# Twenty cache copies move from behind the output projection's weights into the compression stage

## The reference, cut to what matters

```python
kv_all = jnp.concatenate([bufs[g], qkv[:, :, g, 1:3]], axis=1)
new_bufs.append(kv_all[:, kv_all.shape[1] - keep:])
```

## Time and profile before

| what | value |
|---|---|
| three runs | 1793.05, 1796.68, 1798.58 us (median 1796.68) |
| the profiled execution | 1787.76 us, its span 1786.1 us |
| TensorE busy | 1573.9 us (88%), mean granted clock 0.942 |
| VectorE, ScalarE, GpSimd busy | 661.4, 389.7, 203.4 us |
| HBM read, written | 413.88 MB, 192.48 MB |
| share of SP's copy line (L499) in the chain that ended last | 10% |

### The profile page before, as it was taken

One profiled execution on the slowest core, in us unless ns is written; L12 is line 12 of the kernel. 1 busy time (PEld: TensorE's weight loads), 2 busy tenths in 40 slices (PEclk: granted clock), 3 DMA queues, 4 the chain that ended last, 5 costly groups with the idle time before them and its releaser, 6 DMA issues.

```text
span 1786.1 us, 23452 instructions
## 1 busy us (share of the span) xinstructions
PE 1573.9 (88%) x8593; PEld 1276.7 (71%) x8593; DVE 661.4 (37%) x1526; ACT 389.7 (22%) x1179; POOL 203.4 (11%) x301
## 2 busy tenths in 40 slices
PE   6999998999899999999999999999776800889996
PEld 5877787668788888878888878676544600778885
DVE  2256412158823210036767631554655200112001
ACT  1111111133320000026666511453322100000001
POOL 1100000112401000001111100453242000000000
PEclk8899999999999999989999999998899855999998
DMA  5599999999779976687999423201588999999740
GB/s 172 207 354 381 408 383 342 376 366 333 250 142 257 315 253 235 208 137 116 145 139 145 127 76 108 95 1 48 199 300 281 350 329 328 369 373 375 292 141 24
DMA packets 170946, 423.33 MB, mean 237 GB/s; under 512 B 10376, under 2 KB 131536, under 8 KB 168032
## 3 DMA queue, kind: packets, MB, share of 16 engines
q1 hardware_dynamic: 147840, 344.27, 59.2%
q0 software_dynamic: 19312, 67.47, 14.2%
q10 hardware_dynamic: 3696, 10.32, 1.6%
HBM read 413.88 MB, written 192.48 MB: 339 GB/s over the span
## 4 chain that ended last, share of the span: by engine, by line
PE 70%; SPq 12%; DMA 7%; DVE 6%; issue 2%; ACT 1%; POOL 0%; ACTq 0%; DVEq 0%; POOLq 0%
PE bank L621 18%; PE bank L787 13%; SPq L499 10%; PE bank L774 9%; PE bank L703 4%; PE bank L806 2%; PE bank L857 2%; PE bank L854 2%; PE bank L859 2%; DMA a_win_sample<-oT 2%; PE bank L714 2%; PE bank L658 2%; DMA cring<-cache_b_kv 1%; PE bank L751 1%; DMA a_win_sample<-area 1%
## 5 line engine op out<-in xcount | busy, mean ns | idle before, releaser
L621 PE MATMUL bank<-hT,wring 128*128 128x264 f32 (+1 forms) x1488 | 353.7, 393 | 0.5 <-DVE area L1333 0.5
L774 PE MATMUL bank<-hT,wring 128*128 128x264 f32 x1024 | 232.8, 390 | 108.1 <-DMA wring<-mlp_w_up 108.1
L621 PEld LDWEIGHTS bank<-hT,wring 128*128 128x128 f32 (+1 forms) x1488 | 279.1, 192 | 66.8 <-issue 8.2
L774 PEld LDWEIGHTS bank<-hT,wring 128*128 128x128 f32 x1024 | 195.3, 192 | 145.5 <-issue 104.4
L787 PE MATMUL bank<-area,wring 128*128 128x264 f32 x1024 | 228.4, 386 | 2.8 <-DVE area L1285 2.8
L787 PEld LDWEIGHTS bank<-area,wring 128*128 128x128 f32 x1024 | 194.6, 190 | 36.6 <-DVE area L1283 3.6
L1649 ACT ACTIVATE turned<-xT 128x264 f32<-128x264 f32 x40 | 16.9, 423 | 649.9 <-DVE xT L1289 565.1
L1283 DVE SCALAR_TENSOR_TENSOR area<-bank,rv 128x264 f32 x64 | 27.7, 432 | 274.7 <-PE bank L774 274.4
L1289 DVE TENSOR_TENSOR xT<-bank,xT 128x264 f32<-128x264 f32 x16 | 6.9, 432 | 220.3 <-PE bank L787 220.3
L562 POOL TENSOR_SCALAR area<-ident,small 128x128 f32<-128x128 f32 x96 | 56.3, 603 | 179.9 <-DVE small L1366 179.9
L621 PE MATMUL bank<-oT,wring 128*128 128x264 f32 x256 | 61.9, 400 | 0.9 <-DVE oT L1630 0.5
(11 more groups left out here) (311 smaller groups left out, 2319.6 us busy)
## 6 DMA issues: line engine op xcount, KB each, us to landing
a_win_sample<-cache_a_win SPq DMA_DIRECT2D x64, 2047.0 KB, 21.3
wring<-a_w_in SPq DMA_DIRECT2D x36, 1024.0 KB, 13.4
wring<-mlp_w_up SPq DMA_DIRECT2D x32, 1024.0 KB, 13.4
wring<-mlp_w_down SPq DMA_DIRECT2D x32, 1024.0 KB, 5.1
a_win_sample<-cache_a_win SPq DMA_DIRECT2D x16, 2044.0 KB, 20.2
cring<-cache_a_win POOLq DMA_DIRECT2D x24, 1024.0 KB, 11.3
cring<-cache_b_kv POOLq DMA_DIRECT2D x62, 256.0 KB, 6.5
cring<-cache_b_kv SPq DMA_DIRECT2D x50, 256.0 KB, 7.6
```

The source lines that it names most:

```text
L621: mm = pe.matmul(bk[half if bank is None else bank][0:width, 0:R], wring[:, blk % NW, c, half * P:half * P + width], rhs[:, c, :], start=( ...
L774: mm = pe.matmul(bk[half][:, 0:R], wring[:, blk % NW, c, half * P:(half + 1) * P], hT[:, c, :], start=(c == 0), stop=(c == DC - 1))
```

## The change

The copies are issued by a small function, `copies(n)`. After each of SP's eight page groups it takes 3 copies (groups 0 to 3) or 2 (groups 4 to 7) from the list: 12 + 8 = 20. The 20 behind block 86 are gone. The list and its order are the same; so are the last 26 copies, one behind each block from 87 to 112. No wait on a semaphore is added or removed, and no copy is added or left out.

```diff
+            def copies(n):
+
+                for d, s in shifts[:n]:
+                    sp.dma_start(d, s).then_inc(S["copies_done"], 16)
+                del shifts[:n]
+
             def w_block(i):
...
                     cmp_loads(sp, i, range(SP_PAGES), ks_landed)
+                    copies(3 if i < 4 else 2)
                     continue
...
                 elif B_UP0 <= i < B_BIN:
                     n_copies = 1 if i % 3 == 0 else 0
                 else:
-                    n_copies = {B_UP0 - 1: 16, B_UP1 - 1: 20}.get(i, 1 if i >= B_UP1 else 0)
-                for d, s in shifts[:n_copies]:
-                    sp.dma_start(d, s).then_inc(S["copies_done"], 16)
-                del shifts[:n_copies]
-            while shifts:
-                d, s = shifts.pop(0)
-                sp.dma_start(d, s).then_inc(S["copies_done"], 16)
+                    n_copies = {B_UP0 - 1: 16}.get(i, 1 if i >= B_UP1 else 0)
+                copies(n_copies)
+            copies(len(shifts))
```

## The result

The changed kernel takes 1721.2 us (median of four executions, 1712.99 to 1767.02) against 1797.4 us before; the ratio is 0.9565, with a 95% interval from 0.9513 to 0.9617. It is 76 us faster. Some executions of both kernels and of most variants run at a lower granted clock and take longer, so the ratios and the lists of times in the experiments leave them out, and single traces are compared by stages in front of the attention of layer B, where that clock showed (this stretch took 395 to 433 us in four of the traces, 355 to 372 us in the others).

What follows compares the result with a forecast made beforehand. Bound: 20 copies queued on SP ahead of block 87, for which PE idles 99.0 us; DMA engines full in the compression. -112.9 + 79 + 12 = -22 us against the median 1796.7 gives 1775 us, range 1722 to 1803.

Steps and rivals of the forecast that it cites:

- part 1: MLP 1: with the 20 copies gone from behind block 86, its work takes MLP 0's time, -112.9 us.
- the lead of 25 us: MLP 1: block 87 issued 25.2 us before needed; ten large copies shrink this to about 12 us, so nothing waits.
- Part 3: MLP 0: three copies behind page group 0 delay weights up to block 46, 18 - 6 = +12 us of PE wait.
- Part 2: Compression: 15 copies behind page groups 1 to 6 cost 90 us of engine time, partly given back; sum +79 us.
- so I let times add: Compression: DMA engines taken as full (share 1.05, queues 49% each), so copies' 6.0 us each add to the pages' time.
- the hidden rival: Compression: if bytes are the limit, all copies fit beside the pages; 5 to 25 us come back, 1690 to 1709; chance 0.12.
- PE's lower clock after waits: Compression: idle gaps of 11 to 17 us lower PE's clock; hidden in groups 1 to 6, about 4 us in group 7.
- The 8 us given back for POOL's turns: Compression: POOL's page packets in q0 still get turns while copies run in q1, 30 of an engine's 280, about 8 us.
- The 8 us for POOL's window loads: Compression, group 7: POOL's 4 MB window loads take turns with SP's last pages, adding about 8 us.
- The rival in which copies cost over 7.5 us each: Page groups: copies ahead spread the engines; above 7.5 us each the kernel is over 5 us slower; chance 0.14.

## Why the prediction was wrong

**What bounded the kernel, and part 1, were right.** Block 87 stood behind twenty copies, and MLP 1 now runs at the pace of MLP 0: 113.93 us for the up product in one piece, 113.2 us won against 112.9 predicted. A copy behind each block does no harm, as the lead of 25 us said.

**Part 3 was right in size, and only half in its reason.** The three copies behind group 0 cost 12.0 us in this trace, as summed, and PE's largest wait for weights there is 7.2 us, for block 46 as named. That the figure agrees to the digit is luck, given 4 us of scatter in this stretch. And with spread pages the same three copies cost nothing, so the room was taken by the slow pages as much as by the copies.

**Part 2 failed, in one step: "so I let times add", with the pages' time left as it was.** It took the DMA share of 1.05 at 164 GB/s, and the two queues at 49% each, for engines without room, and put the copies' time on top of the pages' 29.3 us. What the runs showed in its place: a page packet's time there is no fixed price. Its packets are held up at their destination of 16 partitions; written to 128 partitions, the same packets need 42% of the engines' time instead of 98%. And with copies among them pages move faster than pages alone, even while no copy is under way. The changed kernel shows both halves. From 862 to 876 us, beside POOL's pages:

```profile
DMA packets 217, 4.91 MB, mean 351 GB/s; under 512 B 51, under 2 KB 51, under 8 KB 146
...
q1 hardware_dynamic: 114, 4.54, 92.7%
q0 software_dynamic: 101, 0.35, 8.9%
```

Pages with no copies under way: from 972 to 984 us of the changed kernel, then from 877 to 897 us of the kernel before:

```profile
DMA packets 976, 2.44 MB, mean 203 GB/s; under 512 B 145, under 2 KB 145, under 8 KB 975
```

```profile
DMA packets 1184, 2.99 MB, mean 150 GB/s; under 512 B 176, under 2 KB 176, under 8 KB 1183
```

So the copies do take the engines nearly for themselves, and at the price that was summed (4.54 MB in 92.7% of 14 us are 6.0 us for a copy of 2.1 MB); it is the pages' term that shrank. An estimate from these rows: 4.16 MB of pages at 203 to 233 GB/s (877 to 889 us) are 18 to 20.5 us, and a copy is 5.6 to 6.4 us. Three copies then make 35 to 40 us a group, two 29 to 33, four 40 to 46. Measured from group 3 on were 36.1 and 38.3 us with three, 33.4 and 29.3 with two, and 37.9 to 46.8 with four. (One group of 40.2 us in the kernel with two a group lies outside.) The page groups on SP start 33 to 38 us apart where PE waits, not 40 to 47.

The term was +79 us and measured +19.5: 12.8 us of waits of PE (36.0 - 32.1, 38.3 - 31.6, 33.4 - 31.2 in the stages), the rest is PE at a lower clock after each wait (32.1, 31.6 and 31.2 us busy against 29.3) and 1.7 us in the first group, less the 1.6 us that it waited for pages before. (The 1.7 us need not be the copies': with only the three behind group 0 that group takes 45.6 us too.)

I had the sign of it in hand. The prediction set out, for the hidden rival, that POOL's pages and weights together moved 173 GB/s where two page streams reached 139, and gave it 0.12. That rival had a right sign, that some of a page's time is not the engines' own, and the end of its range, 1725 us, holds the measured time. But it let the copies fit beside unchanged pages up to 373 GB/s; the groups with copies reach 286 to 334. The Trainium skill's figure of about 358 GB/s for HBM (DMA: Bandwidth & Descriptors, "Bandwidth"), which I set against the share in the trace, is nearer to what the stage does (355 GB/s with spread pages) than the share was. It is no ceiling in this case, where a stage moved 373 GB/s.

**The smaller terms of part 2.** PE's lower clock after waits is there (0.91 in two groups), and PE is busy 7 us longer over three groups with it; whether the time would fall by as much without it was not tested. The 8 us given back for POOL's turns do not come out of their rows: 30 packets of an engine at 0.37 us (48.9% of 30 us for 40 packets) are 11 us. The 8 us for POOL's window loads I see no sign of: the rows from group 5 on have no wait. The rival in which copies cost over 7.5 us each is out; fifteen copies cost 1.3 us each on average, net of what the pages gained.

**Still open.** Why pages go faster after a copy is not shown. That copies put the 16 engines out of step, so that they write different pages to different partitions, fits all one-queue runs and the stretch in which no copy is under way, but the records do not show which engine writes where at what time. It is argued only. That PE waits for groups 2 to 4 and for none later (where groups also have fewer copies) fits the same picture (the landing improves from group to group), and was not tested by itself.

## What to carry to other kernels

A DMA share near 1 says that packets are under way, not that engines have no room: divide bytes by time and compare with the best rate elsewhere in the same trace. If it is far below (here 142 against 373 GB/s), ask what the packets wait for at their destination, and do not take the time that they need now for a fixed term of a sum. Copies between HBM and HBM in such a stage cost less than their own time (here 1.3 us each for 6), but not nothing: two a group still cost 12 us with two queues and 3 us with one, against the stage of the kernel before. And a large batch of copies should not stand in a queue ahead of weights that PE needs next; here it cost 99 us of PE's time.

## What the runs showed of the hardware that I had not expected

- The same 2 KB and 4 KB packets took 98% of the engines' time when each page went to 16 partitions, and 42% when it went to 128.
- Pages alone in one queue moved 121 to 133 GB/s. With one copy behind each group the queue moved 187 to 253 GB/s, with two 259 to 318, and the pages themselves landed sooner.
- Pages went faster even after the copies had landed: 215 GB/s against 128 in one queue, 203 against 150 in two.
